# A stick-breaking attention layer: attention in units of four steps, scores and turns in 64-row tiles, projections in groups of 256 tokens

## The reference

```python
def stick_breaking_attention(q, k, v):
    ...
        z = jnp.einsum('bthd,bshd->bhts', q[:, t0:kend], k[:, :kend]).astype(jnp.float32) * scale
        mask = s_idx < t_idx
        log_beta = jax.nn.log_sigmoid(z)
        log_rem = jnp.where(mask, jax.nn.log_sigmoid(-z), 0.0)
        after = lax.cumsum(log_rem, axis=3, reverse=True) - log_rem
        w = jnp.where(mask, jnp.exp(log_beta + after), 0.0)
        outs.append(jnp.einsum('bhts,bshd->bthd', w.astype(v.dtype), v[:, :kend]))

def mixer_stick_breaking(h, w_in, w_out):
    proj = jnp.einsum('bsd,de->bse', h, w_in)
    q, k, v, g = jnp.split(proj, 4, axis=-1)
    ...
    return jnp.einsum('bse,ed->bsd', o * jax.nn.silu(g), w_out)

x = x + mixer_stick_breaking(rmsnorm(x, a_norm[j]), a_w_in[j], a_w_out[j])
return rmsnorm(x, final_norm)
```

## Time and profile before

| | |
|---|---|
| median of 3 runs | 1651.9 us (1651.38 to 1653.42) |
| time of the profiled execution | 1651.07 us |
| its span in the profile | 1649.3 us |
| busy: PE, PEld | 1638.1 us (99%), 1376.1 us (83%) |
| busy: DVE, ACT, POOL | 1348.6 us (82%), 904.7 us (55%), 165.5 us (10%) |

### The profile page before, as it was taken

One profiled execution on the slowest core, in us unless ns is written; L12 is line 12 of the kernel. 1 busy time (PEld: TensorE's weight loads), 2 busy tenths in 40 slices (PEclk: granted clock), 3 DMA queues, 4 the chain that ended last, 5 costly groups with the idle time before them and its releaser, 6 DMA issues.

```text
span 1649.3 us, 23497 instructions
## 1 busy us (share of the span) xinstructions
PE 1638.1 (99%) x8642; PEld 1376.1 (83%) x8642; DVE 1348.6 (82%) x1901; ACT 904.7 (55%) x1782; POOL 165.5 (10%) x200
## 2 busy tenths in 40 slices
PE   9999999999999999999999999999999999999998
PEld 7888878888888888888888888888888888888887
DVE  5536369989898999899998999898889899957874
ACT  6625245655665566656565655656566656743221
POOL 0020020110111011101110211012011101000000
PEclk9999999999999999999999999999999999999999
DMA  9858643343424252434333333425242424779722
GB/s 314 276 163 277 190 142 108 110 126 92 150 68 136 69 154 80 132 94 124 109 98 106 120 113 90 132 87 147 58 147 81 144 77 129 247 259 363 247 105 87
DMA packets 164370, 237.10 MB, mean 144 GB/s; under 512 B 49952, under 2 KB 91936, under 8 KB 164256
## 3 DMA queue, kind: packets, MB, share of 16 engines
q1 hardware_dynamic: 94912, 160.29, 31.5%
q10 hardware_dynamic: 69344, 75.32, 14.6%
HBM read 155.78 MB, written 79.76 MB: 143 GB/s over the span
## 4 chain that ended last, share of the span: by engine, by line
PE 96%; DMA 2%; ACT 1%; DVE 0%; POOL 0%; issue 0%; SPq 0%; DVEq 0%
PE proj_ps L764 31%; PE turn_ps L794 15%; PE o_ps L810 8%; PE o_ps L812 8%; PE z_ps L784 8%; PE z_ps L782 8%; PE proj_ps L713 5%; PE turn_ps L851 3%; PE o_ps L713 3%; PE turn_ps L713 3%; PE z_ps L851 3%; PE proj_ps L851 2%; PE o_ps L851 1%; DMA gate<-gate_cols 1%; POOL w_raw L697 0%; DMA w_raw<-in_w_qkg 0%
## 5 line engine op out<-in xcount | busy, mean ns | idle before, releaser
L1003 ACT ACTIVATE u<-z_ps 128x512 f32<-128x512 f32 (+3 forms) x640 | 341.6, 534 | 365.4 <-PE z_ps L784 362.3
L1236 DVE TENSOR_TENSOR_SCAN u<-u,u 128x512 f32<-128x512 f32 x384 | 492.1, 1281 | 0.0
L1241 DVE TENSOR_TENSOR r_turned_lo<-turn_ps,r_turned_hi 128x512 fp32r<-128x512 f32 (+3 forms) x640 | 380.9, 595 | 103.5 <-ACT r_turned_hi L1009 99.5
L1009 ACT ACTIVATE r_turned_hi<-turn_ps 128x512 fp32r<-128x512 f32 (+3 forms) x640 | 341.0, 533 | 96.7 <-PE turn_ps L794 45.2
L794 PE MATMUL turn_ps<-ident,u 128*128 128x128 f32 x2176 | 352.6, 273 | 0.0
L764 PE MATMUL proj_ps<-hT_hi,w_hi 128*128 128x512 f32 x768 | 317.9, 414 | 0.0
L764 PE MATMUL proj_ps<-hT_hi,w_lo 128*128 128x512 f32 x768 | 317.7, 414 | 0.0
L764 PE MATMUL proj_ps<-hT_lo,w_hi 128*128 128x512 f32 x768 | 317.5, 413 | 0.0
L794 PEld LDWEIGHTS turn_ps<-ident,u 128*128 128x128 f32 x2176 | 266.8, 140 | 54.5
L697 POOL TENSOR_SCALAR w_raw<-w_raw,a_norm_col 128x128 f32<-128x128 f32 x192 | 163.7, 871 | 1201.3 <-DMA w_raw<-in_w_qkg 1201.3
L784 PE MATMUL z_ps<-k_parts,q_swapped 128*128 128x512 f32 (+3 forms) x640 | 235.8, 368 | 0.0
(11 more groups left out here) (138 smaller groups left out, 1601.1 us busy)
## 6 DMA issues: line engine op xcount, KB each, us to landing
qk_hi_cols<-made_hi ACTq DMA_DIRECT2D x64, 256.0 KB, 2.8
qk_lo_cols<-made_lo ACTq DMA_DIRECT2D x64, 256.0 KB, 2.7
x_T<-in_xT SPq DMA_DIRECT2D x29, 512.0 KB, 6.0
w_raw<-in_w_qkg SPq DMA_DIRECT2D x24, 512.0 KB, 3.7
x_rows<-in_x SPq DMA_DIRECT2D x16, 512.0 KB, 4.9
v_rows<-v_stage ACTq DMA_DIRECT2D x32, 256.0 KB
v_here<-v_rows SPq DMA_DIRECT2D x64, 128.0 KB, 3.1
v_next<-v_rows SPq DMA_DIRECT2D x64, 128.0 KB, 3.5
```

The source lines that it names most:

```text
L1003: nc.scalar.activation(u_t[(m // CB) % RU][STEPS[m][3]][:, 0:w], z_ps[m % RZ][:, 0:w], ACT.Sigmoid, scale=-Z_SCALE).then_inc(s_u, 1)
L1009: nc.scalar.activation(rt_hi[m % RT][:, 0:w], t_ps[m % RT][:, 0:w], ACT.Copy).then_inc(s_hi, 1)
L1236: nc.vector.tensor_tensor_scan(u, u, other, start, ALU.mult, op).then_inc(s_r, 1)
L1241: nc.vector.tensor_tensor(rt_lo[m % RT][:, 0:w], t_ps[m % RT][:, 0:w], as_f32(rt_hi[m % RT][:, 0:w]), ALU.subtract).then_inc(s_lo, 1)
```

## The change

**Units.** The loops run over slots s of one unit each (160 units, two slots of lead) instead of steps. In slot s PE does, in this order: the scores of steps 0 and 1 of unit s + 2 (`scores_first`), all turns of unit s (`turns`), the scores of steps 2 and 3 of unit s + 2 (`scores_second`), one or two groups of `project`, and `weigh` for the four steps of unit s.

**64-row tiles.** Scores and turns use half of the rows of the array. q_hi, q_lo of even steps lie in rows 0 to 63 and of odd steps in rows 64 to 127; k_hi and k_lo lie in both halves. Two steps are scored together by three matmuls each (hi*hi, lo*hi, hi*lo), in turn for the two halves, into two banks. A 128x128 block of u is turned as two transposes of 64 rows with 64 columns of output each, into the two banks of one pair `turn_ps[p % 2]`; `hi` and `lo` then work on two steps at once (up to 1024 columns).

**Groups of 256 tokens.** The projections have 192 groups of 24 matmuls with 256 columns; they have no bank of their own but take `z_ps[1]` and, where a slot has two groups, `z_ps[2]`. Ten groups are made ahead of attention. The slots -2, -1, every tenth slot and four others (22 in all) have two groups.

**GpSimd.** `weight_lo`, `dif` and `dv_low` move from DVE to POOL, with one pair of buffers for v instead of two.

```diff
@@ groups @@
+    return [(t, 2 * c + f) for t, c in order for f in range(2)]
...
-LEAD_SCORES = 9
-LEAD_TURN = 2
-LEAD_SCAN = 6
-RU, RZ, RT, RO, RP = 3, 2, 3, 2, 2
-BEFORE = 5
-FILL_NUM, FILL_DEN = 6688, 2000
+LEAD = 2
+RU, RO = 3, 1
+HALF = P // 2
+GW = CH // 2
+BEFORE = 10
+def groups_of_slots():
...
+        two = s < 0 or s % (HS // CB) == 0 or s % (4 * HS // CB) == 2 * HS // CB + 4
+        slots[s] = list(range(g, min(g + (2 if two else 1), NG)))
@@ banks @@
-        z_ps = [pb(f"z_ps{n}") for n in range(RZ)]
-        t_ps = [pb(f"turn_ps{n}") for n in range(RT)]
+        z_ps = [pb(f"z_ps{n}") for n in range(3)]
+        turn_ps = [ctx.enter_context(nc.psum_tensor(f"turn_ps{n}", [P, 2, CH], F32)) for n in range(2)]
...
+        p_ps = z_ps[1:]
@@ POOL @@
+                def weight_lo(t, ks):
...
+                    for k in ks:
+                        last = nc.gpsimd.tensor_tensor(w_lo[t % 2][:, k, :], w_raw[t % 2][:, k, :],
+                                                       as_f32(w_hi[t % 2][:, k, :]), ALU.subtract)
+                    nc.gpsimd.tensor_tensor(va[:], vb[:], va[:], ALU.subtract).then_inc(s_dif, 1)
+                    nc.gpsimd.tensor_tensor(dv_head[:, blocks, DH:P], va[:], as_f32(dv_head[:, blocks, 0:DH]),
+                                            ALU.subtract).then_inc(s_dlo, 1)
@@ PE @@
+                def scores(m, banks):
...
+                    for n, (a, b) in enumerate(((q_hi, k_hi), (q_lo, k_hi), (q_hi, k_lo))):
+                        for odd in range(PAIR):
+                            rows = slice(odd * HALF, (odd + 1) * HALF)
...
+                            last = nc.tensor.matmul(banks[odd][:, 0:CH - lo], a[c % 2][rows, tau], b[rows, sig],
+                                                    start=(n == 0), stop=(n == 2))
+                def scores_first(u):
...
+                    if u:
+                        pe.wait_ge(s_u, CB * u)
+                    pe.wait_ge(s_plo, SLOT_GROUPS[u - LEAD - 1][0] + 1 if u else BEFORE)
+                    scores(CB * u, z_ps[0:2])
+                def scores_second(u):
+                    pe.wait_ge(s_u, CB * u + 1)
...
+                    scores(CB * u + PAIR, (z_ps[2], z_ps[0]))
+                def turns(p):
...
+                            for half in range(2):
+                                rows = slice(half * HALF, (half + 1) * HALF)
+                                last = nc.tensor.transpose(turn_ps[p % 2][:, half, at:at + HALF],
+                                                           u_t[m // CB % RU][t][rows, r * P - lo:(r + 1) * P - lo], ident[rows, rows])
...
+                for s in range(-LEAD, NU):
+                    if inside(s + LEAD):
+                        scores_first(s + LEAD)
...
+                        turns(2 * s)
+                        turns(2 * s + 1)
+                    if inside(s + LEAD):
+                        scores_second(s + LEAD)
+                    for n, g in enumerate(SLOT_GROUPS.get(s, [])):
+                        if inside(s + LEAD):
+                            pe.wait_ge(s_u, CB * (s + LEAD) + 2 + n)
+                        project(g)
...
+                        for m in range(CB * s, CB * s + CB):
+                            weigh(m)
@@ ACT @@
+                    if ended is not None:
+                        empty(ended)
+                        store_o(ended)
+                    if inside(s + LEAD):
+                        stick(CB * (s + LEAD))
+                        stick(CB * (s + LEAD) + 1)
+                    if s - 1 in SLOT_GROUPS:
+                        store_low(SLOT_GROUPS[s - 1][-1])
+                    if inside(s):
+                        hi(2 * s)
+                        hi(2 * s + 1)
+                    if inside(s + LEAD):
+                        stick(CB * (s + LEAD) + 2)
+                        stick(CB * (s + LEAD) + 3)
@@ DVE @@
+                for s in range(-LEAD, LAST_SLOT + 1):
+                    if inside(s):
+                        lo(2 * s)
+                        lo(2 * s + 1)
+                    here = SLOT_GROUPS.get(s, [])
+                    for r in range(CB):
+                        if inside(s + LEAD):
+                            scan(CB * (s + LEAD) + r)
+                        if r % 2 == 0 and r // 2 < len(here):
+                            made_low(here[r // 2])
```

More of the change, by code:

```diff
@@ L105, in projection_groups @@
     first, last = number["g", LAST_G], number["g", KT - 1]
[L106 removed]
+    order += [(first, 2), (first, 0), (last, 2), (last, 0), (first, 1), (last, 1), (first, 3), (last, 3)]
+    return [(t, 2 * c + f) for t, c in order for f in range(2)]
 TILES = column_tiles()
@@ L800, in weigh @@
+                def weigh(m):
                     h, c, j, r = STEPS[m]
                     w = turn_width(m)
+                    if c == 0 and r == 0:
+                        pe.wait_ge(s_dlo, NC * h + j + 1)
                     begin, end = j == c and r == 0, j == NC - 1 and r == CB - 1
-                    weights = dv_head[:, j * CB + sigma_block(m), :]
-                    if first:
-                        if c == 0 and r == 0:
-                            pe.wait_ge(s_dlo, NC * h + j + 1)
-                        if begin and NC * h + c:
-                            pe.wait_ge(s_ost, NC * h + c)
-                        pe.wait_ge(s_lo, m + 1)
-                        nc.tensor.matmul(o_ps[:, 0:w], weights, rt_hi[m % RT][:, 0:w], start=begin, stop=False)
-                        return
@@ L812, in weigh @@
-                    last = nc.tensor.matmul(o_ps[:, 0:w], weights, rt_lo[m % RT][:, 0:w], start=False, stop=end)
+                    if begin and NC * h + c:
+                        pe.wait_ge(s_ost, NC * h + c)
+                    p = m // PAIR
+                    if m % PAIR == 0:
+                        pe.wait_ge(s_lo, p + 1)
+                    here = slice(blocks_before(m) * P, blocks_before(m) * P + w)
+                    weights = dv_head[:, j * CB + sigma_block(m), :]
+                    nc.tensor.matmul(o_ps[:, 0:w], weights, rt_hi[p % 2][:, here], start=begin, stop=False)
@@ L813, in weigh @@
+                    last = nc.tensor.matmul(o_ps[:, 0:w], weights, rt_lo[p % 2][:, here], start=False, stop=end)
                     if end:
@@ L854, in put_out @@
                             last.then_inc(s_y, 1)
-                project(0, filled(-LEAD_SCORES - 1))
+                for g in range(BEFORE):
+                    if g < 2:
+                        pe.wait_ge(s_vst, 2 * NB)
+                    else:
+                        pe.wait_ge(s_plo, g - 1)
+                    project(g)
                 pe.wait_ge(s_vfirst, 16)
                 for k in range(KT):
-                    last = nc.tensor.transpose(t_ps[2][:, k * NB:(k + 1) * NB], v_first[:, k * P:(k + 1) * P], ident[0:NB, 0:NB])
+                    last = nc.tensor.transpose(t_ps[3][:, k * NB:(k + 1) * NB], v_first[:, k * P:(k + 1) * P], ident[0:NB, 0:NB])
@@ L1097, in _ @@
                 act.wait_ge(s_wolo, KT)
-                for g in range(2):
+                for g in range(BEFORE):
                     made_high(g)
@@ L1110, in _ @@
                 for v in range(2 * NB - 2, 2 * NB):
                     v_stored(act, v)
-                for n in range(-LEAD_SCORES, LAST_PIECE_STEP + 1):
-                    ended = chunk_end(n - 1) if inside(n - 1) else None
+                for s in range(-LEAD, LAST_SLOT + 1):
+                    ended = chunk_end(s - 1) if inside(s - 1) else None
                     if ended is not None:
                         empty(ended)
-                    if inside(n + LEAD_SCORES):
-                        stick(n + LEAD_SCORES)
-                    if ended is not None:
```

423 lines of the change are left out of this document (193 added, 230 removed).

## The result

The changed kernel takes 1702.5 us (median of 4 runs, 1700.8 to 1704.9), the kernel before 1652.2 us in the same session (1651.4 to 1653.4). The ratio is 1.0305, with a 95% interval of 1.0287 to 1.0323: 3% slower, where the prediction had 1641 and "faster" as the likelier sign. 1702 lies inside its range.

The account below looks back on a forecast made before the run. PE was taken as the bound, busy for 99% of the span. The terms -53 - 96 + 22 + 2 + 28 + 72 + 10 + 5 = -10 took 1651.07 to 1641 us, range 1555 to 1720.

Parts of the forecast that it names:

- scores, halves side by side: PE's scores: the two 64-row matmuls of a pair run together and cost one interval, -53 us.
- turns: PE's transposes of u: a block as two half transposes costs 0.066 us instead of 0.11, -96 us.
- projections: PE's projection groups in the loop: 24 matmuls per 256 tokens cost 2.88 us, +22 us.
- changes of rows, and first matmuls: PE switching between 64-row and 128-row use, two per slot: 0.09 us each, +28 us, bounds 0 and 51.
- ACT's wait at chunk ends: Second scores in 63 slots: ACT's two DMA issues delay the first `stick`, PE waits 1.15 us each, +72 us.
- ten groups ahead: Projections ahead of attention: +2 us of matmuls, +10 us waiting for low parts to land in single buffers.
- waits in the slots -2 and -1: Lead slots: no turns or `weigh` hide the waits of the first and second scores, +5 us.
- irregular waits in the other slots, half clock with them: Attention loop: one group per slot of 7 us or more covers the stores, so no cost.
- GpSimd and VectorE: Moved work on GpSimd and VectorE's load: no cost while PE bounds; a rival, chance 0.05, had 1708 us.
- rival 4: Scores and turns: the 64-row halves don't run side by side at all, 1995 us, chance 0.05.
- rival 2: Turns: only one weight load runs at a time, 0.118 us per block, 1723 us in all, chance 0.17.
- The sign is wrong: Closing test of "faster": fails if turns exceed 0.073 us per block or ACT's two issues don't delay the `stick`.

Follow-up runs that it names:

- e6: Changed kernel with w_lo of the loop's weight tiles made by VectorE in one operation each instead of by GpSimd: 1700.9 us, ratio 1.0303.
- e2: Changed kernel with one extra small matmul over 64 rows behind each projection group: 1783.4 us.
- e3: Changed kernel with one extra small matmul over all 128 rows behind each projection group: 1731.0 us.
- e9: Changed kernel with the two stores at chunk ends issued by SyncE instead of ScalarE, and two buffers for made_lo: 1649.2 us, ratio 0.9985.
- e10: e9 with w_hi one slot later on ScalarE and w_lo made by VectorE 10 steps behind the load: 1635.7 us, ratio 0.9909.

## Why the prediction was wrong

Its sum was -10 and the spans differ by +51: 61 us are missing. Term by term:

| term | forecast | measured |
|---|---|---|
| scores, halves side by side | -53 | as forecast but for the first pair (below) |
| turns | -96 | -109 (0.060 a block and not 0.066) |
| projections | +22 | as forecast (0.12 apart) |
| changes of rows, and first matmuls | +28 | 160 x 0.51 = +82 |
| ACT's wait at chunk ends | +72 | 63 x 1.16 = +73 |
| ten groups ahead | +12 | +8 (first scores 220.07, 211.87 before) |
| waits in the slots -2 and -1 | +5 | +7 (21.9 us instead of 15) |
| irregular waits in the other slots, half clock with them | 0 | +32 |
| GpSimd and VectorE | 0 | 0 for `w_lo` (e6), not measured for the rest |

**The step that failed** is the term "changes between 64-row and 128-row use": the interval of the earlier trace rows gave 0.09, and that part is right to 0.01. But the row shows only the time to the next start. The first matmul behind a change also takes 0.11 longer, and so does the first pair of scores behind the turns, which needs no change. Per slot that is 2 x 0.09 + 3 x 0.11 = 0.51 us, 54 us more than the 28. The rows of the kernel before had this price too: "four turns and one matmul take 0.68" in the earlier trace rows was read as four turns and a matmul of 0.23, but that matmul, the first behind the turns, takes 0.32 to the next start. The sum of the kernel before came out all the same, since the 0.09 went into the 0.11 of a turn; for the changed kernel nothing carried it. The prediction's upper bound of 51, and with it the Trainium skill's rule that a change of the tiling mode drains the engine (TensorEngine Tiling (Array Packing), Key Properties), pointed the right way; the runs put 0.14 us on a change among short matmuls (e2 against e3) and 0.20 on one behind long ones.

**A second step failed:** "In the loop one group comes per slot of 7 us or more, so the stores are covered." The median landing is 2.4 us but the longest 7.8, as the longest was before (2.3 to 7.9, median 2.7, when VectorE waited for it once, 3.4 us). With one buffer for `made_lo`, two groups in some slots, and ScalarE's store of a low part ahead of `hi`, each slow landing or late weight tile comes through to PE. e9 and e10 show it: two buffers for `made_lo`, a later w_hi and w_lo on VectorE gave 25 us, clock included. Forecast were 5 us in two slots, measured are 7 there and 32 in the others. The clock is part of it: that PE runs at 0.50 for some microseconds behind some of these waits was in no term.

The two add to 54 + 34 = 88. Against them stand 13 us of turns that were cheaper than forecast and 4 of the ten groups; ACT's wait was 1 more. That makes 72. The forecast's intervals add up to 1248 us for the loop before, which took 1254; the 6 us missing there come off the 72. That leaves 66 against the 61 that were missing, 5 us that the runs don't settle.

**What held:** the halves run side by side (rival 4 out); a block costs 0.06 us and not 0.118 (rival 2 out), and for that the loads of the two halves must overlap as well; ACT's two issues are on PE's path, with 1.16 us of wait a slot; VectorE is not the bound. By the Trainium skill (TensorE: Matmul & The Clock Gate, Part 3) a load overlaps a running matmul only when the row groups differ. The trace differs: the projections' loads use the same 128 rows as the matmul ahead and run beside it (a load at 705.07 for 0.19, beside the matmul from 704.96 to the next start at 705.18). By the Trainium skill (SBUF — State Buffer, SBUF: two separate sides) GpSimd's two-input work should lock VectorE out. The trace agrees (the scan of 1.79 us above), but the time does not hang on it: taking 176 such operations away changed the scans by 12 ns on average and the time by nothing. "The sign is wrong if turns cost more than 0.073 per block, or if ACT's two issues don't delay the stick" was too short a list: neither happened, and the sign was wrong.
